# Ten weight loads without a product on TensorE after each round of attention heads and HGRN2

## The chip, the cores and the metric

The kernel runs on one core of a Trainium2 chip. The metric is the device time of one execution in microseconds (us): the median over several runs. TensorE has two clock levels, 2.4 GHz, which the profile calls a granted clock of 1.0, and 1.2 GHz, a granted clock of 0.5; a stretch that mixes them shows a value between.

## The reference

A hybrid model over 512 tokens of width 1024, all in float32. The first block has two layers; the second block (two more layers with gated feed-forward parts, pooling and dilated attention) isn't touched by the change. One layer of the first block:

```python
h = rmsnorm(x, norm1_g[l])
u = jnp.einsum('btd,de->bte', h, w_in[l])            # all projections at once
y_m = mlstm_mixer(mq, mk, mv, mo, mi, mf, ...)       # 4 heads
y_a = diff_attention(aq, ak, av, ...)                # 4 heads of two softmaxes, causal
y_h = hgrn2_mixer(hq, hf, hi, hg, ...)               # 4 heads, a gated linear recurrence
mix = jnp.concatenate([y_m, y_a, y_h], axis=-1)
x = x + jnp.einsum('bte,ed->btd', mix, w_out[l])
h2 = rmsnorm(x, norm2_g[l])
a = jnp.square(jax.nn.relu(jnp.einsum('btd,df->btf', h2, w_up[l])))
x = x + jnp.einsum('btf,fd->btd', a, w_down[l])
```

The differential attention takes, per head, two causal softmaxes of q k^T and applies their difference to v. HGRN2 is, per head, a product of q and k with a decay between the two positions, applied to v, plus the state carried from earlier positions.

## The kernel before

Everything is kept transposed, with channels on the 128 partitions and the 512 tokens along the free dimension, and the residual x stays on the chip. A dense projection is cut into units of weights of up to 128 x 2048 elements. Each weight is split into a high and a low part (ScalarE rounds at L577, GpSimd subtracts at L594), and TensorE makes three products per tile (L661, L662, L663) in place of one exact one. The five engines each run a program of their own, written out in order; they meet at semaphores only. What `self.pe.e` issues runs on TensorE in the order of issue. A float32 or bf16 product is issued as a weight load and a product, so each product brings its own weights. In the profile an exact float32 product issued by the helper `mm` (L418, its work at L419) shows as two records.

The order is made by Python generators. Each part of the model is a generator per engine that yields between its steps; `weave` (L258) takes so many steps of each of its streams per round and yields once per round; `often` (L289) goes through a generator and lets three of four steps end a round, so that it advances four steps in three rounds; `run` (L296) exhausts a generator. The same Python runs for all engines, each time with that engine's generators.

`mixers` (L2621) weaves two lines in each of the two layers. The first line ends the mLSTM and then runs attention heads 1 and 3 (`heads(1, ...)`). The second line first runs the last ten units of the input projection (`rest`), and when these are over it weaves heads 0 and 2 (`other_heads`) with `states`: HGRN2, and then the output projection (`out`). So from the end of `rest` on, heads 1 and 3, heads 0 and 2 and HGRN2 share the engines with no dense projection beside them, until `out` begins. On TensorE these are

- `pe_heads` (L1814): the reciprocal norms spread with `sel` (L1831), v turned to tokens (L1836), and for each of four query blocks the scores q k^T (L1846), a bf16 identity times a causal mask added to them (L1848), the weights turned (L1856), the weights times v (L1862); then sums with a column of ones (L1868) and factors spread (L1876);
- `pe_hgrn` (L2021): the values turned to tokens (L2034), q k^T (L2042), seven levels of decayed products (L2055, tiles called scr), the keys turned (L2068), the near part (L2076), the state carried over blocks (L2082, L2086), and the norm (`pe_rstd`, L1315).

VectorE and ScalarE do the steps between: for HGRN2 a level's product is copied under a mask by VectorE (L2154), and the decayed operand of a next one is made by VectorE (L2132, L2133, L2141, L2142) around an exponential on ScalarE (L2218); for the heads VectorE takes maxima (L1899) and combines the two softmaxes (L1908, L1911), and ScalarE takes the exponentials (L1964).

`ident16` (L409) is the bf16 identity, 128 x 128, made once at the start (L1216) and used as weights for the masks.

Of the kernel before, what the change touches and what calls it, by code (L numbers as in the profile page):

```python
# [257 lines left out]
def weave(*streams):  # L258

    streams = list(streams)  # L260
    while streams:
        for s in list(streams):
            for _ in range(s[1]):
                if next(s[0], s) is s:
                    streams.remove(s)
                    break
        yield


def every(n, steps):  # L270
    for i, _ in enumerate(steps):
        if i % n == n - 1:
            yield


def chain(*parts):
    for steps in parts:
        yield from steps


def beside(n, steps, *others):

    for i, _ in enumerate(steps):
        if i % n == n - 1:
            for line in others:
                next(line, None)


def often(steps):  # L289

    for i, _ in enumerate(steps):
        if i % 4 != 1:
            yield


def run(steps):  # L296
    for _ in steps:
        pass
# [19 lines left out]
class Kernel:  # L318
# [2299 lines left out]

    def mixers(self, l, rest, mlstm, heads, hgrn, out):  # L2621


        first = PHASES[f"in_ah{l}"].first
        mine = FIRST_BANK[first + PHASES[f"in_ah{l}"].count]
        self.heads_begun = False
        self.heads_left = 2

        def first_line():
            yield from mlstm  # L2630
            while self.unit < first + 6:
                yield
            self.heads_begun = True
            yield from heads(1, (5, 6, 7))
            self.heads_left -= 1

        def states():
            yield from hgrn((mine, mine + 1))
            for i, _ in enumerate(out):
                yield  # L2640

                while i == 11 and self.heads_left:
                    yield

        def other_heads():
            yield from heads(0, (2 - mine, 3 - mine, 4))
            self.heads_left -= 1

        def second_line():
            yield from every(3, rest)  # L2650
            line = states()
            while not self.heads_begun:
                yield next(line)
            yield from weave((other_heads(), 1), (often(line), 1))
        run(weave((first_line(), 1), (second_line(), 1)))

    def tensor(self):
        self.pe_start()
        for l in range(DEPTH):
            mlstm = self.pe_mlstm(l)  # L2660
            beside(3, chain(self.pe_dense(f"in_m{l}"), self.pe_dense(f"gates{l}"), self.pe_dense(f"in_n{l}")), mlstm)
            self.mixers(l, self.pe_dense(f"in_ah{l}"), mlstm, lambda n, banks: self.pe_heads(l, n, banks),
                        lambda banks: self.pe_hgrn(l, banks), self.pe_dense(f"out{l}"))
            for g in range(2):
                run(self.pe_dense(f"up{l}{g}"))
                run(self.pe_dense(f"down{l}{g}"))
        for name in ("gateupa0", "backa0", "gateupa1", "backa1"):
            run(self.pe_dense(name))
        self.pe_post_norm()
        for name in ("pool_in", "pool_out"):  # L2670
            run(self.pe_dense(name))
            if name == "pool_in":
                self.pe_last_groups()
        self.pe_post_norm()
        for name in ("gateupb0", "backb0", "gateupb1", "backb1"):
            run(self.pe_dense(name))
        self.pe_post_norm()
        for name in ("k", "v", "gateupc0", "backc0", "gateupc1", "backc1"):
            run(self.pe_dense(name))
        self.pe_post_norm()  # L2680
        self.attention_b(self.pe_dense("q"), self.pe_dilated)
        self.pe_weights()
        run(self.pe_dense("o"))
        self.pe_post_norm()
        for name in ("gateupd0", "backd0", "gateupd1", "backd1"):
            run(self.pe_dense(name))
        self.pe_post_norm()
        self.pe_store()
# [151 lines left out]
```

## Time and profile before

| | |
|---|---|
| median of 3 runs | 3642.12 us (3635.84 to 3644.48) |
| the profiled execution | 3640.93 us |
| its span | 3639.6 us |
| TensorE busy, its weight loads | 94%, 75% of the span |
| VectorE, ScalarE, GpSimd busy | 35%, 31%, 34% |
| chain of waits: TensorE, VectorE, ScalarE | 85%, 9%, 3% |
| mean granted clock | 0.953 |

The profile is one execution. Its page gives the busy time of each engine, the same in 40 equal slices with the granted clock, the DMA queues, the chain of work that ended last and the costliest groups of instructions. The trace behind it was asked for windows (busy time in a stretch), the timeline (instructions in order of time), the waits and the chain of a stretch. PE is TensorE's products and PEld its weight loads, which overlap the products; DVE is VectorE, ACT ScalarE, POOL GpSimd, and L419 is line 419.

### The profile page before, as it was taken

How to read it: one execution, taken by the hardware profiler on the slowest of the kernel's cores; microseconds unless marked ns; L12 is line 12 of the kernel's file. 1: busy time of each engine (PE TensorE's matmuls, PEld its weight loads, DVE VectorE, ACT ScalarE, POOL GpSimd, SP SyncE). 2: the span in 40 equal slices, each digit the busy share in tenths (PEclk: the TensorE clock that was granted, in tenths of full speed). 3: DMA queues.
4: the chain of work that ended last, by engine and by line, in shares of the span. 5: the costliest groups of instructions: out<-in, count | busy, mean ns of one | idle time of the engine just before them, and what ended most of it. 6: DMA issues, size and time to landing. Idle time of an engine off the chain costs nothing.

```text
span 3639.6 us, 37143 instructions
## 1 busy us (share of the span) xinstructions
PE 3403.8 (94%) x15674; PEld 2725.1 (75%) x15674; DVE 1256.4 (35%) x2031; ACT 1139.0 (31%) x1557; POOL 1223.6 (34%) x299
## 2 busy tenths in 40 slices
PE   7996799999987999999998999999999989769999
PEld 5675588887755788888887778887888867658887
DVE  5336531314356421222123441123221243662122
ACT  3234432323234432322223332223221233433222
POOL 4220144443210344444444324443444432024442
PEclk9996899999987899999999999999999999879998
DMA  4110023332210133333333223333433323023332
GB/s 125 58 58 1 24 94 104 93 93 84 63 35 1 59 103 93 93 94 97 99 91 104 78 70 93 104 93 114 140 91 102 89 81 110 12 58 93 100 93 74
DMA packets 461820, 296.76 MB, mean 82 GB/s; under 512 B 14296, under 2 KB 454158, under 8 KB 461598
## 3 DMA queue, kind: packets, MB, share of 16 engines
q1 hardware_dynamic: 453664, 277.09, 26.2%
q10 hardware_dynamic: 7990, 17.30, 1.4%
q8 instruction: 123, 2.02, 0.3%
q14 instruction: 43, 0.35, 0.0%
HBM read 285.97 MB, written 8.39 MB: 81 GB/s over the span
## 4 chain that ended last, share of the span: by engine, by line
PE 85%; DVE 9%; ACT 3%; POOL 1%; issue 1%; DMA 0%; SPq 0%; DVEq 0%; ACTq 0%; POOLq 0%
PE bank L661 24%; PE bank L662 24%; PE bank L663 24%; PE bank L419 9%; PE bank L703 1%; PE bank L704 1%; PE bank L705 1%; DVE scr L2154 1%; DVE ta L1513 1%; DVE x L1120 1%; DVE ta L1118 1%; POOL wlo L594 0%; DVE qkv L2432 0%; DVE ta L2429 0%; DVE tb L2430 0%
## 5 line engine op out<-in xcount | busy, mean ns | idle before, releaser
L594 POOL TENSOR_TENSOR wlo<-raw,whi 128x2048 fp32r<-128x2048 f32 (+3 forms) x278 | 1178.3, 4239 | 2331.8 <-ACT whi L577 2331.8
L661 PE MATMUL bank<-xh,whi 128*128 128x512 f32 x2304 | 916.8, 398 | 23.2 <-DVE xl L1144 15.3
L663 PE MATMUL bank<-xh,wlo 128*128 128x512 f32 x2304 | 900.4, 391 | 0.0
L662 PE MATMUL bank<-xl,whi 128*128 128x512 f32 x2304 | 900.3, 391 | 0.0
L577 ACT ACTIVATE whi<-raw 128x2048 fp32r<-128x2048 f32 (+3 forms) x280 | 493.9, 1764 | 585.1 <-PE bank L663 547.3
L661 PEld LDWEIGHTS bank<-xh,whi 128*128 128x128 f32 x2304 | 434.7, 189 | 141.7 <-issue 32.2
L663 PEld LDWEIGHTS bank<-xh,wlo 128*128 128x128 f32 x2304 | 434.2, 188 | 92.6
L662 PEld LDWEIGHTS bank<-xl,whi 128*128 128x128 f32 x2304 | 435.1, 189 | 87.5 <-issue 1.4
L661 PE MATMUL bank<-ah,whi 128*128 128x512 f32 x1216 | 474.1, 390 | 5.2 <-POOL wlo L594 5.2
L662 PE MATMUL bank<-al,whi 128*128 128x512 f32 x1216 | 473.8, 390 | 0.0
L663 PE MATMUL bank<-ah,wlo 128*128 128x512 f32 x1216 | 473.6, 389 | 0.0
L850 DVE TENSOR_TENSOR ta<-bank,rs 128x512 f32<-128x512 f32 x176 | 120.9, 691 | 594.7 <-PE bank L663 594.4
L661 PEld LDWEIGHTS bank<-ah,whi 128*128 128x128 f32 x1216 | 228.7, 188 | 53.5 <-POOL wlo L594 6.0
L663 PEld LDWEIGHTS bank<-ah,wlo 128*128 128x128 f32 x1216 | 228.7, 188 | 47.8
L662 PEld LDWEIGHTS bank<-al,whi 128*128 128x128 f32 x1216 | 228.7, 188 | 47.3
L661 PE MATMUL bank<-mh,whi 128*128 128x512 f32 x480 | 188.1, 392 | 9.6 <-DVE ml L1649 9.6
L1083 ACT ACTIVATE ah<-ta 128x512 fp32r<-128x512 f32 x88 | 55.9, 635 | 433.5 <-DVE ta L854 433.5
L662 PE MATMUL bank<-ml,whi 128*128 128x512 f32 x480 | 187.7, 391 | 0.0
L663 PE MATMUL bank<-mh,wlo 128*128 128x512 f32 x480 | 187.7, 391 | 0.0
L832 DVE TENSOR_TENSOR x<-bank,x 128x512 f32<-128x512 f32 x48 | 33.2, 691 | 313.8 <-PE bank L663 313.8
L419 PE MATMUL bank<-u 64*128 64x128 f32 (+5 forms) x576 | 104.7, 387 | 26.0 <-ACT u L2211 16.4
L1080 ACT ACTIVATE tb<-ta 128x512 f32<-128x512 f32 x88 | 55.7, 633 | 224.3 <-DVE ta L850 224.2
(378 smaller groups left out, 3227.0 us busy)
## 6 DMA issues: line engine op xcount, KB each, us to landing
raw<-in_ffn_w_gate SPq DMA_DIRECT2D x85, 512.0 KB, 4.0
raw<-in_ffn_w_up SPq DMA_DIRECT2D x85, 512.0 KB, 5.2
raw<-in_w_up SPq DMA_DIRECT2D x64, 512.0 KB, 4.7
raw<-in_w_down SPq DMA_DIRECT2D x64, 512.0 KB, 5.1
raw<-in_w_in SPq DMA_DIRECT2D x56, 512.0 KB, 4.8
raw<-in_ffn_w_down SPq DMA_DIRECT2D x64, 384.0 KB, 4.1
raw<-in_ffn_w_down SPq DMA_DIRECT2D x64, 320.0 KB, 3.8
raw<-in_w_out SPq DMA_DIRECT2D x16, 512.0 KB, 4.4
```

Of the source, the lines that this page charges most:

```text
L419: return self.pe.e.matmul(out, lhsT, rhs, start=start, stop=stop, skip_group_check=True)
L577: a.e.activation(self.whi[slot][:, 0:n], self.raw[slot][:, 0:n], ACT.Copy).then_inc(self.hi_made.tick(u), 1)
L594: g.e.tensor_tensor(self.wlo[slot][:, 0:n], self.raw[slot][:, 0:n], self.whi[slot][:, 0:n].bitcast(F32), ALU.subtract).then_inc(self.lo_ma ...
L661: pe.e.matmul(bank, hi[:, at:at + P], xh, start=k == ks[0], stop=False)
L662: pe.e.matmul(bank, hi[:, at:at + P], xl, start=False, stop=False)
L663: last = pe.e.matmul(bank, lo[:, at:at + P], xh, start=False, stop=k == ks[-1])
L703: pe.e.matmul(bank, hi[:, at:at + P], xh, start=k == 0, stop=False)
L704: pe.e.matmul(bank, hi[:, at:at + P], xl, start=False, stop=False)
L705: last = pe.e.matmul(bank, lo[:, at:at + P], xh, start=False, stop=k == ph.nk - 1)
L850: v.e.tensor_tensor(r[:], bank[:], self.rs[:], ALU.mult).then_inc(read, 1)
L1080: a.e.activation(self.tb[0][:], self.ta[0][:], ACT.Silu).then_inc(self.part_a.tick("silu", u), 1)
L1083: a.e.activation(self.ah[:, j, :], self.ta[1][:], ACT.Copy).then_inc(self.part_a.tick("hi", u), 1)
```

## The change

After each round of the outer weave of `mixers`, if HGRN2 has begun and has not ended, TensorE loads the bf16 identity as weights ten times. No product follows these loads. Only TensorE's program passes the function in; for the other engines `between` is None and `alone` has no effect.

```diff
+    def pe_keep_awake(self):
+        for _ in range(10):
+            self.pe.e.ldweights(self.ident16())
+
-    def mixers(self, l, rest, mlstm, heads, hgrn, out):
+    def mixers(self, l, rest, mlstm, heads, hgrn, out, between=None):
...
         self.heads_left = 2
+        self.alone = False
...
         def states():
+            self.alone = True
             yield from hgrn((mine, mine + 1))
+            self.alone = False
             for i, _ in enumerate(out):
                 yield
...
-        run(weave((first_line(), 1), (second_line(), 1)))
+        for _ in weave((first_line(), 1), (second_line(), 1)):
+            if between and self.alone:
+                between()
...
             self.mixers(l, self.pe_dense(f"in_ah{l}"), mlstm, lambda n, banks: self.pe_heads(l, n, banks),
-                        lambda banks: self.pe_hgrn(l, banks), self.pe_dense(f"out{l}"))
+                        lambda banks: self.pe_hgrn(l, banks), self.pe_dense(f"out{l}"), self.pe_keep_awake)
```

## Rows read from the trace of the kernel before

**Rows 1.** The page: span, busy time, slices, instruction loading, the chain by engine.
```profile
span 3639.6 us, 37143 instructions
PE 3403.8 (94%) x15674; PEld 2725.1 (75%) x15674; DVE 1256.4 (35%) x2031; ACT 1139.0 (31%) x1557; POOL 1223.6 (34%) x299
...
PEclk9996899999987899999999999999999999879998
...
q8 instruction: 123, 2.02, 0.3%
...
PE 85%; DVE 9%; ACT 3%; POOL 1%; issue 1%; DMA 0%; SPq 0%; DVEq 0%; ACTq 0%; POOLq 0%
```

**Rows 2.** Windows of both stretches: length, busy time per engine, granted clock, DMA.
```profile
core 0: us, PE busy (x) PEld busy (x) DVE busy (x) ACT busy (x) POOL busy (x), PEclk, DMA share, GB/s
266.30:420.30 154.00, 105.98 (x633) 75.50 (x632) 94.58 (x234) 67.22 (x146) 0.00 (x0) 0.70 0.00 1
1051.10:1205.20 154.10, 106.06 (x633) 75.03 (x632) 94.58 (x234) 67.21 (x146) 0.00 (x0) 0.71 0.00 1
```

**Rows 3.** The chain within 266.3 to 420.3 us: shares, then start, length, what.
```profile
by line: PE bank L419 39.6%; DVE scr L2154 7.4%; DVE tiny L1899 4.3%; issue 4.3%; DVE u L1911 3.8%; PE bank L1856 3.3%; PE bank L1836 2.5%; DVE scr L2142 2.1%; ACT scr L2218 2.0%; DVE tiny L1908 1.9%; DVE scr L2141 1.6%; DVE scr L2132 1.6%;
...
293.71 6.14 PE bank L419 x40
```

**Rows 4.** TensorE's longest wait within 266.3 to 420.3 us: total, times, longest.
```profile
PE bank L419 <- DVE scr L2154: 19.9, 9, 4.8
```

**Rows 5.** Timeline of the products: start, length, what, in brackets idle time before.
```profile
293.71 2.08 PE L419 MATMUL bank<-scr 64*128 64x128 f32 x16 [1.26 <-DVE scr L2154]
295.72 2.07 PE L419 MATMUL bank<-u 128*128 128x128 f32 x8
297.73 2.08 PE L419 MATMUL bank<-scr 64*128 64x128 f32 x16
299.60 0.96 PE L419 MATMUL bank<-u 64*128 64x384 f32 x4
...
301.77 1.16 PE L419 MATMUL bank<-scr 64*128 64x128 f32 x16
307.69 0.59 PE L419 MATMUL bank<-scr 64*128 64x128 f32 x2 [4.76 <-DVE scr L2154]
```

**Rows 6.** The same at the end of the first stretch.
```profile
420.35 0.77 PE L661 MATMUL bank<-mh,whi 128*128 128x512 f32 x1 [4.81 <-DVE ml L1649]
```

**Rows 7.** Loads of the bf16 identity: timeline; then all, min/median/max in ns.
```profile
286.32 0.11 PEld L419 LDWEIGHTS bank<-half 128*128 128x128 bf16 x2 [0.62 <-issue]
...
3030.19 0.45 PEld L419 LDWEIGHTS bank<-half 128*128 128x128 bf16 x8
...
3115.18 0.77 PEld L419 LDWEIGHTS bank<-half 128*128 128x128 bf16 x8 [0.22 <-issue]
...
L419 PEld LDWEIGHTS bank<-half x184: 95/98/152, 269.1 to 3183.5; 128*128 128x128 bf16 x184
```

**Rows 8.** Float32 loads with one-column products: timeline; then all, min/median/max in ns.
```profile
2472.44 0.97 PEld L419 LDWEIGHTS bank<-ones,tb 128*128 128x128 f32 x8 [0.74 <-ACT tb L1101]
...
L419 PEld LDWEIGHTS bank<-ones,tb x48: 186/192/337, 1966.1 to 3621.1; 128*128 128x128 f32 x48
```

**Rows 9.** Windows, as rows 2: three stretches, each followed by the one behind it.
```profile
404.70:409.10 4.40, 3.92 (x34) 3.80 (x33) 0.17 (x1) 3.15 (x5) 0.00 (x0) 1.00 0.02 4
409.20:413.30 4.10, 2.55 (x6) 1.17 (x7) 1.94 (x10) 3.82 (x7) 0.00 (x0) 0.50 0.00 0
381.90:385.90 4.00, 2.31 (x14) 0.83 (x12) 3.49 (x8) 2.29 (x7) 0.00 (x0) 1.00 0.00 0
386.00:392.80 6.80, 6.11 (x50) 4.97 (x50) 2.88 (x9) 2.07 (x6) 0.00 (x0) 1.00 0.00 1
2470.80:2474.10 3.30, 2.03 (x17) 1.83 (x15) 0.99 (x3) 2.12 (x3) 1.26 (x1) 1.00 0.21 50
2474.20:2477.50 3.30, 2.07 (x8) 1.78 (x8) 1.16 (x2) 0.00 (x0) 0.00 (x0) 0.50 0.75 261
```

## The prediction

> **What bounds the kernel now.** The page comes first [rows 1]: TensorE is busy for 94% of the span and the chain of work that ended last is 85% TensorE, nearly all of it dense projections at a granted clock of 1.0. The change touches none of those. The digits of the granted clock dip twice, at slices 3 to 4 and 11 to 13. The windows [rows 2] cut out the two stretches behind these dips, one per layer, in which the last attention heads and HGRN2 run with no projection beside them: 266.3 to 420.3 us and 1051.1 to 1205.2 us. In each, TensorE is busy for 106 of 154 us at a mean granted clock of 0.70 and 0.71, VectorE for 95. So the whole question lies in 308 of 3640 us, and the second stretch repeats the first to 0.1 us. The chain inside the first stretch [rows 3] gives TensorE 39.6 + 3.3 + 2.5 = 45%, and most of the rest is VectorE in short steps. TensorE idles for the other 48 of the 154 us; the largest part of that, 19.9 us in nine waits, is for VectorE's masked copies of HGRN2 [rows 4]. The stretch is bounded by a relay: a TensorE group, a VectorE group, a TensorE group. An extra microsecond on TensorE ahead of a group in that relay is a microsecond more; inside a wait it is free.
>
> **The change, part by part.** It removes and moves nothing. It adds ten weight loads of a bf16 identity after each round of the weave in which HGRN2 has started and not ended. It adds no wait, no semaphore, no DMA, and only TensorE's program has it.
>
> How many: HGRN2's TensorE generator yields 42 times for each of its two pairs of heads, 8 times in the norm and twice at its end, 94 in all. `often` takes four of its steps in three rounds, so this is 70 rounds. 70 x 10 = 700 loads per layer, 1400 in the run. The program grows by 1400 on 37143 instructions, 4%; instruction loading takes 0.3% of the DMA engines [rows 1], so I cost this at nothing, and nothing waits on that queue.
>
> Where they stand: I laid the rounds of the code beside TensorE's groups of the first stretch. 50 groups of products are issued in it, and the first dense product behind it makes 51. In front of 19 of the 51 TensorE waits at least 0.58 us; the other 32 follow the group ahead within 0.2 us. The groups of [rows 5] show the pattern: the scr group at 293.71 ends a round, a round with no product follows, so two rounds of loads (20) come before the u group at 295.72; one round comes before the u group at 299.60 and one before the scr group at 301.77, all three without idle time. Ahead of 307.69 stand two more rounds, and there TensorE idles 4.76 us for VectorE, which hides them. Over the stretch, 41 of the 70 rounds of loads stand ahead of the 32 groups with no idle time, and 29 fall into waits. For 25 of the 41 the chain of waits runs through TensorE at that moment (as in the piece of 6.14 us at 293.71 [rows 3], which holds the two and the one); at the other 16 it runs on VectorE or ScalarE. The last round falls into the 4.81 us wait ahead of the first output projection [rows 6].
>
> What one load costs: no row shows a load with no product behind it. The nearest [rows 7]: two bf16 loads start 15 ns apart, since the pair takes 0.11 us and one takes 0.10; eight with a product each take 0.45 us, so (0.45 - 0.10) / 7 = 50 ns on average, and the seven of steady pace are 56 ns apart, which the product sets; at the half clock eight take 0.77 us, 95 ns each. The median length of one is 98 ns. So a load takes between 15 ns (only its issue) and about 100 ns (its whole length, if each must end before the next begins). Below nothing is not possible for the load itself; a gain could come only through the clock, and that is a rival. I take 35 ns, the middle between 15 and the 56 at which a load and a product together run, because the rows at full clock already show loads overlapping: 98 ns long and 56 apart. Ten loads then cost 0.35 us.
>
> A rule of the Trainium skill bears on this. TensorE: Matmul & The Clock Gate, section LDWEIGHTS (loading the stationary operand), puts a load at its columns over 1.2 GHz; by it this would be an estimated 107 ns, the end of rival B. [...]
>
> The sum: 25 rounds on the chain paid in full, and half of the 16 off it (a late TensorE group there delays VectorE's in-order queue in some places and not in others), 33 x 0.35 = 11.6 us per layer, 23 us for both. No waited group overflows: the largest pile is three rounds, 1.05 us, ahead of waits of 1.7 us and more. From 420.3 us on everything keeps its pace, only later. The profiled execution took 3640.9 us, 1.2 under the median of 3642.1. **3640.9 + 23.1 = 3664 us.**
>
> **Rivals.**
>
> A, the forecast, over its load prices of 25 to 56 ns: from 25 x 0.25 x 2 = 12.5 to 41 x 0.56 x 2 = 46 us, so 3653 to 3687 us.
>
> B, loads in series: with no product between them each waits for the last. Then ten cost 1.0 us. The 25 rounds on the chain plus what overflows the short waits come to 27 us per layer, all 41 plus the overflow to 43: 3696 to 3726 us. It speaks for it that a bf16 load is 95 ns long at the least [rows 7]; against it that f32 loads with one-column products, which add next to no product time, come eight in 0.97 us though one is 192 ns long, so they start (0.97 - 0.19) / 7 = 111 ns apart and overlap [rows 8].
>
> C, the loads nearly free: at 15 ns ten cost 0.15 us, 25 x 0.15 x 2 = 7.5 us, and some of that is absorbed where VectorE is late anyway. 3641 to 3652 us, mostly inside the noise. For it: the issue spacing in [rows 7].
>
> D, faster: the loads keep the granted clock at its upper level (2.4 GHz) through the stretch. A scr group of 16 takes 2.08 us at 0.5 and 1.16 us at 1.0 [rows 5], 44% less. TensorE has 45% of 154 us on the chain, 70 us, of which 60% runs at 0.5 (mean clock 0.70): 42 x 0.44 = 18.5 us per layer, 37 for both, less 7 to 28 us for the loads: 3611 to 3632 us. Against it stand [rows 9]. From 404.7 to 409.1 us TensorE counts as busy for 3.92 of 4.4 us, with loads for 3.80 of them, 16 of the 34 products having one column; the stretch behind it runs at 0.5. From 381.9 to 385.9 it is busy for 2.31 of 4.0 us, with loads for 0.83 but longer products, and the stretch behind it stays at 1.0. From 2470.8 to 2474.1, 15 loads in 1.83 us with one-column products, behind dense work at 1.0, end at 0.5. So products hold the clock, and loads alone did not. These loads are f32; a bf16 load might count otherwise, and that is what is left of D. The same page of the Trainium skill, Part 1, says that the clock follows how busy the engine was and advises against idle gaps; read plainly, that gives D, and these rows speak against that reading for weight loads.
>
> E, the change doesn't do what it says, because `alone` is set too early or late: it is false while the projections run and true from HGRN2's first step on, so I give this nothing.
>
> **How the numbers follow.** A 57%, C 18%, B 15%, D 10%. The predicted time is A's, 3664 us. The range goes from 3640 (C with everything absorbed) to 3708 (the middle of B); outside lie D and half of B, 18%. A measurement of this kernel can tell about 0.3%, 11 us, from no change: D is faster (0.09 with its small end left out), C and the lowest edge of A are the same (0.22), the rest is slower (0.69).
>
> **What would show each step.** In the profile after: 1400 loads more from the identity at the new line, and TensorE's count of products unchanged. The spacing of ten loads in a row: 0.35 us says A, 0.15 C, 1.0 B. The two stretches longer by 11 to 12 us each and the time between them unchanged at 631 us. The mean granted clock still 0.68 to 0.73 in both; 0.9 or more would be D. TensorE's waits for the masked copies shorter by some 0.35 to 0.7 us each, not gone. The prediction is wrong if the stretches are shorter, if the loads cost over 60 ns each, or if a stretch grows by less than 8 us at loads of 35 ns, which would mean that VectorE's relay absorbs more than I gave it.

## The result and the profile after

The changed kernel takes 3674.87 us (median of 3 runs, 3673.54 to 3677.03) against 3642.12 us before: ratio 1.0092, 95% interval 1.0078 to 1.0107, 33 us slower. Forecast were 3664 us, range 3640 to 3708. The direction and the range hold; of the 33 us the prediction's sum had 23.

The page of the profile after, the lines that answer to [rows 1]:

```profile
span 3673.6 us, 38543 instructions
PE 3431.1 (93%) x15674; PEld 2798.2 (76%) x17074; DVE 1256.8 (34%) x2031; ACT 1138.7 (31%) x1557; POOL 1223.6 (33%) x299
...
PEclk9996799999976899999999999999999999879999
...
q8 instruction: 129, 2.11, 0.3%
```

1400 loads more and not one product more, and yet TensorE's products are busy for 27 us longer. The same work takes longer, and that was not in the forecast. The windows of the two stretches and of the dense work between them and behind them, columns as in [rows 2]:

```profile
core 0: us, PE busy (x) PEld busy (x) DVE busy (x) ACT busy (x) POOL busy (x), PEclk, DMA share, GB/s
267.40:437.50 170.10, 118.38 (x632) 110.29 (x1324) 94.44 (x234) 67.62 (x146) 0.00 (x0) 0.63 0.00 1
437.60:1066.20 628.60, 620.48 (x2720) 489.56 (x2729) 204.03 (x271) 197.66 (x227) 231.58 (x51) 0.99 0.29 85
1066.20:1236.30 170.10, 118.44 (x632) 110.33 (x1325) 94.50 (x234) 67.63 (x146) 0.00 (x0) 0.63 0.00 1
1236.40:3673.60 2437.20, 2339.27 (x10696) 1918.65 (x10696) 750.39 (x1120) 721.78 (x929) 909.48 (x220) 0.97 0.31 91
```

Each stretch grew from 154 to 170 us, 16 us each, 32 for both; the time between them is 2 us shorter and the time behind them 3 us longer. VectorE's and ScalarE's busy times are those of before. TensorE's products in the stretch are busy for 118 us in place of 106, and the mean granted clock is 0.63 in both, where it was 0.70 and 0.71.

The loads themselves, all of them and then four rows of the timeline in the part that answers to [rows 5]:

```profile
L2623 PEld LDWEIGHTS <-half x1400: 95/102/181, 266.9 to 1230.2; 128*128 128x128 bf16 x175
...
298.59 0.99 PEld L2623 LDWEIGHTS <-half 128*128 128x128 bf16 x20 [0.22 <-issue]
303.54 0.53 PEld L2623 LDWEIGHTS <-half 128*128 128x128 bf16 x10 [0.22 <-issue]
307.66 0.51 PEld L2623 LDWEIGHTS <-half 128*128 128x128 bf16 x10
...
331.26 0.46 PEld L2623 LDWEIGHTS <-half 128*128 128x128 bf16 x10
```

Ten loads take 0.46 us where the clock is 1.0 and 0.53 where it is 0.5; without the length of the last, (0.46 - 0.10) / 9 = 40 ns and (0.53 - 0.10) / 9 = 47 ns from start to start. A round of ten loads so takes TensorE 0.40 to 0.47 us, 0.44 on average. The products around them:

```profile
296.58 2.08 PE L419 MATMUL bank<-scr 64*128 64x128 f32 x16
299.53 2.08 PE L419 MATMUL bank<-u 128*128 128x128 f32 x8 [0.87 <-issue]
301.53 2.08 PE L419 MATMUL bank<-scr 64*128 64x128 f32 x16
304.08 1.65 PE L419 MATMUL bank<-u 64*128 64x384 f32 x4 [0.47 <-issue]
...
308.19 1.16 PE L419 MATMUL bank<-scr 64*128 64x128 f32 x16 [0.23 <-issue]
313.70 1.66 PE L419 MATMUL bank<-scr 64*128 64x128 f32 x12 [4.35 <-DVE scr L2154]
```

Both prices are in these rows. Where [rows 5] has no idle time, TensorE's products now stand apart by 0.87 us behind two rounds of loads and by 0.47 and 0.23 us behind one ("issue": it waits for nothing but its own queue). And the u group at 304.08 takes 1.65 us where it took 0.96: before, the clock had risen to 1.0 by then, now it is still 0.5. The wait for VectorE at the end has shrunk from 4.76 to 4.35 us. The wait of 1.26 us that stood ahead of the first group of [rows 5] is gone: that group, now at 296.58, follows without idle time. Over the stretch the waits of [rows 4] shrank from 19.9 us in nine to 14.8 us in seven, and issue became a line of its own:

```profile
PE bank L419 <- DVE scr L2154: 14.8, 7, 4.3
PE bank L419 <- issue: 6.5, 17, 0.9
```

Laid product by product beside the stretch before, the growth splits into three parts: 12 us more in which products are busy (118 in place of 106), about 12 us more idle time at places where there had been little or none, and about 8 us less at the places where TensorE had waited 0.55 us or more. The first part comes with the lower clock, since the products are the same; the second is the loads; the third says that the waits took back a good part of both. That is bookkeeping on one timeline, and it doesn't say from which of the two the waits took. Which loads are on the path, and what the clock takes, needed experiments.

### The profile page after: what moved, and what is told of

Read it like the earlier page. It is cut to its first block, busy times and chain, and to the rows that moved or that the text cites. A ratio compares the mean times of both kernels' runs of the same rounds, so it can differ in the third digit from the quotient of the medians.

```text
span 3673.6 us, 38543 instructions
## 1 busy us (share of the span) xinstructions
PE 3431.1 (93%) x15674; PEld 2798.2 (76%) x17074; DVE 1256.8 (34%) x2031; ACT 1138.7 (31%) x1557; POOL 1223.6 (33%) x299
## 4 chain that ended last, share of the span: by engine, by line
PE 86%; DVE 9%; ACT 3%; issue 1%; POOL 1%; DMA 0%; SPq 0%; DVEq 0%; ACTq 0%; POOLq 0%
PE bank L661 24%; PE bank L662 24%; PE bank L663 24%; PE bank L419 10%; PE bank L703 1%; PE bank L704 1%; PE bank L705 1%; DVE ta L1513 1%; DVE x L1120 1%; DVE ta L1118 1%; POOL wlo L594 0%; DVE scr L2154 0%; DVE qkv L2432 0%; DVE ta L2429 0%; DVE tb L2430 0%
## 5 line engine op out<-in xcount | busy, mean ns | idle before, releaser
L419 PE MATMUL bank<-u 64*128 64x128 f32 (+5 forms) x576 | 114.0, 417 | 33.4 <-ACT u L2211 12.4
```

Source lines behind the costliest of these rows:

```text
L419: return self.pe.e.matmul(out, lhsT, rhs, start=start, stop=stop, skip_group_check=True)
```

## The experiments

Two theories stood against each other. The first: a load costs 40 to 47 ns where TensorE has no wait to put it in, and besides the loads thin out the products (they leave fewer of them in a given time), so that the granted clock is at 0.5 for longer. The rival: the loads' own time is all. Unless it is said otherwise the edit is to the changed kernel, and all kernels compute the full result.

### How the cost grows with the number

```diff
-        for _ in range(10):
+        for _ in range(5):      # five_loads
+        for _ in range(20):     # twenty_loads
```

> Five loads after each round in place of ten. Theory 1 (loads of 40 to 47 ns on TensorE's path, and a lower granted clock because the products stand thinner): the 41 rounds ahead of groups without idle time cost 0.20 to 0.24 us each, 8 to 10 us per layer; 2 to 4 of it are absorbed and the clock costs up to 5: 12 to 26 us slower than before in all. Rival (only the loads' own time counts, the clock costs nothing): half of the 33 us of ten loads, 16 us.

> Twenty loads after each round. Theory 1: 41 rounds x 0.80 to 0.94 us = 33 to 39 us per layer, the short waits overflow by 1 to 2 us, the clock costs about the 5 us that it costs with ten, and 4 to 5 us are absorbed: 65 to 80 us slower than before, and the time at the half clock longer again. Rival (only the loads' own time): twice 33 us, 66 us, with the time at the half clock growing only as the stretch does.

Five loads: ratio 1.0040 (1.0028 to 1.0053), 14 us. Twenty: 1.0204 (1.0188 to 1.0219), 73 us. With 33 us for ten this is nearly a straight line, so it can't tell the theories apart; both had forecast it. The windows of the stretches do more. Of five loads, then of twenty:

```profile
267.40:428.10 160.70, 113.17 (x632) 92.59 (x977) 94.53 (x234) 67.33 (x146) 0.00 (x0) 0.67 0.00 1
1059.40:1216.70 157.30, 107.88 (x632) 88.56 (x979) 94.27 (x234) 67.26 (x146) 0.00 (x0) 0.71 0.00 1
```

```profile
267.70:457.30 189.60, 124.78 (x632) 147.23 (x2012) 94.04 (x233) 68.00 (x146) 0.00 (x0) 0.58 0.00 1
1086.40:1276.40 190.00, 124.30 (x632) 146.10 (x2013) 94.06 (x233) 67.88 (x146) 0.00 (x0) 0.59 0.00 1
```

The two stretches with five loads hold the same instructions, and the one at 0.67 is 3.4 us longer than the one at 0.71, with 5.3 us more of busy products. The executions show it too: the two of 3647 and 3648 us have a mean clock of 0.953 over the whole kernel, three of the other four, 3656 to 3660 us, 0.946. With twenty the clock of the stretches falls to 0.58 and 0.59. So time goes with the clock and the clock with the number of loads, which is what the first theory says and the rival doesn't. But the stretch at 0.71 also has five loads after each round: with so few the clock can stay where it was before, and that stretch is only 3.2 us longer than before.

### Where the loads stand

```diff
+        n = 0
         for _ in weave((first_line(), 1), (second_line(), 1)):
             if between and self.alone:
-                between()
+                between(n)
+                n += 1
...
+        if n in self.WAITED:       # loads_in_waits, 29 rounds
+        if n not in self.WAITED:   # loads_no_idle, 41 rounds
+        if n in self.OFF:          # loads_off_chain, 16 of the 41
```

> Ten loads only after the 29 rounds of 70 per layer behind which TensorE waits anyway. Theory 1: they are hidden, 0 +/- 4 us against the kernel before, and the granted clock of both stretches stays at 0.70. Rival (each round of loads costs the same wherever it stands): 33 x 29 / 70 = 14 us slower. Rival (loads in the waits hold the clock): faster by 10 us or more, granted clock above 0.75.

> Ten loads only after the 41 rounds per layer behind which TensorE goes on without waiting. Theory 1: nearly the whole of the change, 28 to 34 us slower than before, granted clock near 0.63 in both stretches. Rival (each round costs the same wherever it stands): 33 x 41 / 70 = 19 us slower.

> Ten loads only after the 16 rounds per layer that stand ahead of groups without idle time, at moments when the chain of waits runs on VectorE or ScalarE. The prediction counted half of them: 16 x 0.43 us x 0.5 = 3.4 us per layer, 7 us in all. Rival (off the chain is free): 0 +/- 3 us. Rival (every round ahead of a group without idle time pays in full): 16 x 0.43 = 6.9 us per layer, 14 us in all.

The 29 rounds ahead of waits: ratio 1.0000 (0.9990 to 1.0010). They are 580 more instructions, so a longer program alone costs nothing that can be seen. The 41 others: 1.0097 (1.0082 to 1.0112), 33 us by the medians, the whole change. The 16 of those at moments when the chain of waits is on another engine: 1.0005 (0.9996 to 1.0014), nothing clear of noise, where the expectation had 7 us. The first stretch of that kernel:

```profile
266.30:420.30 154.00, 106.81 (x633) 81.82 (x792) 94.44 (x234) 67.42 (x146) 0.00 (x0) 0.70 0.00 1
```

It has the length and the clock of before. A load costs by its place. By subtraction the 25 rounds per layer on the chain carry the whole cost; a kernel with only these wasn't run. An estimate of their own time is 25 x 0.44 = 11 us per layer, 22 us in all. It leaves 11 of the 33 us that aren't the loads' own time.

The two stretches of the kernel with loads in waits happen to differ by their clock:

```profile
267.90:418.40 150.50, 101.31 (x633) 84.39 (x922) 94.02 (x233) 67.02 (x146) 0.00 (x0) 0.74 0.00 1
1046.70:1200.70 154.00, 106.15 (x633) 87.36 (x923) 94.65 (x234) 67.19 (x146) 0.00 (x0) 0.71 0.00 1
```

The same work and the same hidden loads, 3.5 us apart at 0.74 and 0.71. This pair and that of five_loads give about 1 us of time for 0.01 of clock. From 0.70 or 0.71 down to 0.63 this would be an estimated 7 to 8 us per stretch, 14 to 16 in all, more than the 11 us left over by the subtraction. One pair speaks against so firm a price: the stretches of loads_no_idle have clocks of 0.66 and 0.63 (the expectation had 0.63 for both) and are equally long, 170 us.

### Does a load count for the clock?

First at the end of each stretch, behind the last round, where the clock is 0.5:

```diff
+        if n == 69:
+            for _ in range(80):     # end_loads
+                self.pe.e.ldweights(self.ident16())
...
+        if n == 69:
+            for _ in range(50):     # end_products
+                self.pe.e.matmul(self.bank[6][:, 3 * P:4 * P], self.ident16(), self.ident16(),
+                                 start=True, stop=True, skip_group_check=True)
```

> No loads but 80 in one row, after the last round of each stretch, inside the wait ahead of the first output projection. Theory 1 (a load doesn't hold the granted clock): 3.2 to 3.8 us of loads, hidden, and the clock is 0.5 when the output projection begins, as before: 0 +/- 3 us. Rival (bf16 loads count as much as products): the clock is 1.0 when it begins, and the some 6 us at 0.5 there are gone, 2 to 3 us per layer faster.

> At the same place 50 bf16 products of the identity with itself, 128 columns each, into a bank that nobody reads at that time, in place of the loads. Theory 1 (products hold or raise the clock, loads don't): 2.8 to 5.4 us of products in the same wait, the clock is 1.0 when the output projection begins, 2 to 6 us faster than before in all. Rival (nothing done there changes the clock, since the engine idled too long ahead of it): 0 +/- 3 us.

Windows of end_loads: the burst, then the product behind it.

```profile
412.40:416.20 3.80, 0.22 (x1) 3.66 (x79) 2.13 (x3) 2.01 (x3) 0.00 (x0) 0.50 0.00 0
416.30:418.50 2.20, 2.07 (x2) 0.53 (x3) 0.04 (x1) 0.43 (x1) 0.00 (x0) 0.50 0.00 0
```

The same of end_products:

```profile
412.40:416.60 4.20, 4.20 (x49) 4.06 (x49) 2.13 (x3) 2.41 (x3) 0.00 (x0) 0.62 0.00 0
416.80:418.30 1.50, 1.18 (x5) 0.29 (x2) 0.29 (x1) 0.00 (x0) 0.00 (x0) 1.00 0.00 0
```

Eighty loads in 3.8 us leave the clock at 0.50, and the two product records behind them take 2.07 us. Fifty products in 4.4 us raise it to 1.0, and the same two take 1.12 us. The products' burst is a little longer, but that isn't the reason: the mean of 0.62 over the window of 4.2 us says that the clock was up for its last 1.0 us, from 415.6 us on, and the loads of the other kernel ran until 416.3 us. Neither gained time: 1.0005 (0.9996 to 1.0014) with loads, and with products 1.0017 (1.0008 to 1.0026), which is 6 us slower and outside of what either theory had forecast. The expectation was wrong about the place. The last round ends between the two last spreading products of HGRN2's norm and not behind both, so the burst delayed the second by 3.7 to 4.4 us, and the clock was back at 0.5 when the output projection began. The wait ahead of that projection shrank from 4.81 to 3.12 us in both, which hid part of it. In the products' profile the second output projection starts only 1 us later than before (1206.1 against 1205.3 us); most of the 6 us lie behind it, in work that the edit doesn't touch:

```profile
1205.30:3639.60 2434.30, 2335.48 (x10696) 1915.68 (x10696) 750.32 (x1120) 722.56 (x929) 909.57 (x220) 0.97 0.31 91
1206.10:3645.20 2439.10, 2340.54 (x10696) 1919.93 (x10696) 750.16 (x1120) 721.74 (x929) 909.32 (x220) 0.97 0.31 91
```

These are the rest of the kernel before and of end_products: the same products, 5 us more of busy time and 5 us more in length. Even ahead of the burst the clock differs for the same instructions: from 266.3 to 412.0 us it is 0.71 in the kernel before and 0.75 in both of these. So the clock also differs where the edits do nothing, and a few us of any of these totals can be that.

Then inside the stretch, in waits, with the clock at 1.0. Both leave out the ten loads per round and put a number of their own ahead of the waits that they fit into:

```diff
+    def product(self, bank):
+        self.pe.e.matmul(self.bank[bank][:, 3 * P:4 * P], self.ident16(), self.half[:, 4, :],
+                         start=bank != 7, stop=bank != 7, skip_group_check=True)
...
+        bank, count = self.FILL.get(n, (0, 0))     # products_in_waits: 36 ahead of the longest wait
+        for _ in range(count):
+            self.product(bank)
...
+        for _ in range(self.FILL.get(n, 0)):       # loads_for_products: 50 there
+            self.pe.e.ldweights(self.ident16())
```

`half[:, 4, :]` is a tile of zeros, made at the start; the bank is one that only TensorE touches at that time.

> No loads; bf16 products of 128 columns (identity times zeros) in waits of the stretch alone, sized to them: 20 ahead of the wait of 2.9 us, 36 ahead of 4.9 us, 4 to 22 ahead of eleven others, 50 at the end; a third of the waits can't be filled, since all banks are in use. What is computed stays the same. Theory 1: the granted clock of both stretches rises from 0.70 to 0.80 or more and the kernel becomes faster, by 10 to 30 us. Rival (the clock costs nothing here since VectorE sets the pace): within 5 us of before, whatever the clock.

> The first set of products in waits with each count replaced by 1.4 times as many loads, so that they fill the waits for the same time at 40 ns each (50 loads ahead of the wait of 4.9 us), and none at the end. Theory 1: the clock falls in these waits as before (the group behind the longest wait takes 2.08 us, at 0.5), 0 +/- 4 us. Rival (loads hold a clock that is already up, even if they can't raise it): that group takes 1.16 us, as with products, and the kernel is faster by 5 us or more.

Timeline of products_in_waits, then the loads and the group behind them of loads_for_products:

```profile
302.73 2.18 PE L2630 MATMUL bank<-half 128*128 128x128 bf16 x36
307.48 1.16 PE L419 MATMUL bank<-scr 64*128 64x128 f32 x16 [2.57 <-DVE scr L2155]
```

```profile
303.02 2.06 PEld L2625 LDWEIGHTS <-half 128*128 128x128 bf16 x50
...
307.77 2.08 PE L419 MATMUL bank<-scr 64*128 64x128 f32 x16 [4.68 <-DVE scr L2154]
```

2.2 us of products in the wait hold the clock at 1.0, and the scr group behind it takes 1.16 us; 2.1 us of loads in the same wait don't, and it takes 2.08 us, as in the kernel before. The kernels: loads_for_products 0.9998 (0.9989 to 1.0007), products_in_waits 0.9990 (0.9981 to 0.9999). The latter was expected to gain 10 to 30 us and gained 2 to 4, though its clock rose to 0.74 in both stretches. At the point that the kernel before reaches at 411.8 us it was 3.8 us ahead; then the 50 products at the end took 5.51 us ahead of the second spreading product, and the first output projection started only 0.5 us earlier than before.

### The loads with the clock held up, and the better fill

```diff
+        bank, count = self.FILL.get(n, (0, 0))
+        for _ in range(count):
+            self.product(bank)
+        if n not in self.WAITED:       # products_and_loads; not in more_products_in_waits
+            for _ in range(10):
+                self.pe.e.ldweights(self.ident16())
```

> The same products in waits, and the ten loads after each of the 41 rounds per layer ahead of groups without idle time. It gives the price of the loads at a clock held up. Theory 1: 20 to 30 us slower than the products in waits alone, less than the 33 us that the loads cost without them, since loads start 40 ns apart at the upper clock and 47 at the lower, and nothing more is lost to the clock. Rival (the clock takes no part in the 33 us): 33 us slower than the products alone.

> As the products in waits, without the 50 at the end (which stood ahead of the last spreading product and not in the wait behind it) and with more in the other waits: 62 ahead of the longest, 36, 34 and 8 to 22 ahead of the others. Theory 1 (products hold the clock, a us at the upper clock is worth about a third of a us of time): 8 to 15 us faster than before, clock of both stretches 0.76 or more. Rival (what the clock gives, the added products take): within 4 us of before.

Products in waits and loads in the 41 other rounds: 3663.8 us, 24 us by the medians and 27 us by the ratios over the products in waits alone, where the same loads cost 33 to 35 us without them. Its four runs lie between 3658.5 and 3670.6 us, and the profiled one is the slowest. Windows of the stretches, of products_in_waits and then of this kernel:

```profile
266.30:419.80 153.50, 116.97 (x855) 86.83 (x854) 94.20 (x234) 66.75 (x146) 0.00 (x0) 0.74 0.00 1
1047.90:1201.50 153.60, 117.00 (x855) 86.84 (x855) 94.26 (x234) 66.81 (x146) 0.00 (x0) 0.74 0.00 1
...
268.90:433.30 164.40, 125.70 (x854) 107.70 (x1255) 94.42 (x234) 67.14 (x146) 0.00 (x0) 0.71 0.00 1
1065.00:1232.00 167.00, 126.38 (x854) 108.30 (x1256) 94.53 (x234) 67.33 (x146) 0.00 (x0) 0.70 0.00 1
```

The test was meant to price the loads at a clock held up. It didn't hold it up: the loads took it from 0.74 to 0.70 and 0.71, so the 24 to 27 us have some of the clock in them too. Against the first theory's forecast of 20 to 30 us and the rival's 33 they speak for the first, but they don't split the cost. Between the subtraction (11 us) and the pairs of equal stretches (14 to 16 us, an estimate), the clock took roughly a third to a half of the 33 us, and the loads' own time the rest.

More products, and none at the end: 3627.43 us, ratio 0.9960 (0.9948 to 0.9973), 14 us faster than the kernel before and 47 us faster than the changed one. Its stretches, and the longest wait:

```profile
266.80:413.50 146.70, 112.57 (x897) 83.68 (x896) 93.80 (x234) 66.76 (x146) 0.00 (x0) 0.77 0.00 1
1041.60:1188.30 146.70, 112.61 (x897) 83.71 (x896) 93.83 (x234) 66.79 (x146) 0.00 (x0) 0.77 0.00 1
...
303.27 3.64 PE L2630 MATMUL bank<-half 128*128 128x128 bf16 x62
308.02 1.16 PE L419 MATMUL bank<-scr 64*128 64x128 f32 x16 [1.11 <-DVE scr L2155]
```

154 to 147 us each. So the clock can be raised and time gained, with products in place of loads and in waits only. The products went into 12 of the 29 rounds ahead of waits, into banks that no other engine used at that time.

### What a load's price goes by

```diff
-            self.pe.e.ldweights(self.ident16())
+            self.pe.e.ldweights(self.half[:, 0, 0:32])     # narrow_loads
```

> The change with loads of 32 columns in place of 128. If a load's price is the fixed spacing of 40 ns in the queue, the same as with 128 columns: 33 us slower than before. If it goes with the columns (or what is read): a quarter, 5 to 12 us slower. The loads hold the clock in neither case by theory 1, near 0.63 to 0.70.

Ratio 1.0032 (1.0022 to 1.0041), 9 to 12 us; its ten runs spread from 3647 to 3662 us. Rows of its timeline and of all its loads:

```profile
266.48 0.34 PEld L2623 LDWEIGHTS <-half 128*32 128x32 bf16 x10 [1.50 <-issue]
268.32 0.39 PEld L2623 LDWEIGHTS <-half 128*32 128x32 bf16 x10
...
324.09 0.26 PEld L2623 LDWEIGHTS <-half 128*32 128x32 bf16 x10
...
L2623 PEld LDWEIGHTS <-half x1400: 92/93/163, 266.5 to 1204.2; 128*32 128x32 bf16 x175
```

A load of 32 columns is as long as one of 128, 93 against 102 ns, but the next starts sooner: mostly 15 to 20 ns later at a clock of 1.0 (the row at 324.09: (0.26 - 0.09) / 9 = 19 ns) and 27 ns later at 0.5 (the row at 266.48), and not 40 and 47. Between the two forms the length hardly changes and the spacing does, though not in proportion to the columns.

## Why the prediction was right in direction and short in size

**The place of the question** held: 32 of the 33 us arose in the two stretches, and the dense work kept its pace to 3 us.

**The number and the places** held in the main: 1400 loads, no product more, the 29 rounds ahead of waits free (1.0000), the 41 others the whole cost (1.0097). Three readings were off. The last round doesn't fall into the 4.81 us wait ahead of the output projection but stands ahead of the second spreading product, which now waits 0.46 us for its loads. One wait with three rounds ahead of it is 1.50 us and not 1.7 or more; its 30 loads took 1.46 us and just fitted. And the waits for masked copies didn't all shrink by 0.35 to 0.7 us: the longest did (4.76 to 4.35 us), but two of the nine are gone, one of them 1.26 us long.

**The price of a load** was taken as 35 ns and is 40 to 47. Taking the middle between the issue spacing and the spacing of load and product together [rows 7] was 20% too low; a value nearer to the pair's 56 ns would have been right. The bounds of 15 and 100 ns held it. Over the 25 rounds of both layers this is 4 to 5 us (22 in place of 17.5).

**The half of the 16 rounds off the chain** was wrong. Nothing clear of noise was paid for them (loads_off_chain, 1.0005). The chain of waits had said so, and the prediction hedged against it. This overstated the sum by 16 x 0.5 x 0.35 x 2 = 5.6 us, and it was luck that this hid part of the two terms that were too low.

**The clock** is the step that failed. The prediction weighed whether loads would hold it and rightly said no; [rows 9] had told this, and the bursts at the end and in the long wait confirm it for bf16 loads. From this it went on to a clock unchanged at 0.68 to 0.73 and put its cost at nothing. Measured was 0.63. Where the loads lay off the chain or in waits (loads_off_chain, loads_in_waits) the clock stayed at 0.70 or above; where they stood on the chain it fell, to 0.66 and 0.63 with ten and to 0.58 with twenty. So the thinning of the products is the likely reason. What it cost is a third to a half of the 33 us, by estimates that don't agree better than that. A stretch that already moves between both clock levels has no fixed clock to put into a sum.

So the corrected sum is up to 25 x 0.44 x 2 = 22 us for loads and 11 us or more for the clock. That it comes to the measured 33 proves nothing, since the 11 is what the subtraction left.

**The rivals.** B, loads in series at 1.0 us for ten, is refuted by the spacing. C, nearly free, by the same. D, loads hold the clock, is refuted by the bursts; that a higher clock is worth time was right: products, which do hold it, won 14 us by going from 0.70 to 0.77. The Trainium skill, TensorE: Matmul & The Clock Gate, Part 1, advises against idle gaps; what these runs add is that a gap filled with weight loads still let the clock fall (loads_for_products, 2.08 us for the group behind) or left it low (end_loads, 0.50). For the load itself, the Trainium skill's section LDWEIGHTS (loading the stationary operand) on that page gives an estimated 107 ns. Its section Weight-path perf modes has a faster way to load 128 columns that aren't fp32, with 4 times the speed as the theory for fp8 and about 2 times as measured on trn2; the latter makes an estimated 53 ns. The length of a load in the trace, 102 ns, is near the first figure, and the spacing of 40 to 47 ns is somewhat below the last.

**What stays open.** Why the spacing is 40 to 47 ns for 128 columns wasn't tried further. How the 33 us split between the loads' own time and the clock isn't settled: no run held the clock while the loads stood on the chain, and none had loads in the 25 rounds alone. How much of the clock's fall is chance can't be told from single profiles either. The same kernel's two stretches differ by 3.4 and 3.5 us (five_loads, loads_in_waits), and untouched work by 5 us between kernels (end_products), so each of these splits is good to a few us.

## What to carry to other kernels

Ask of each added instruction whether the chain of waits runs through its engine at that place: 45 of the 70 rounds here were free when tested by themselves, and the cost lay in the 25 others. Where TensorE's granted clock already moves between its two levels, treat it as a result of the change and not as a constant: what spreads the products out can cost twice, once by its own time and once by slower products. To keep the clock up in a wait, fill it with products into an idle bank, sized to the wait, and not with weight loads; here that was worth 14 us of 3641, where the change made the kernel 33 us slower.

## What the runs showed of the hardware

- bf16 weight loads with no product behind them start 40 ns apart at a clock of 1.0 and 47 ns at 0.5 with 128 columns, 15 to 27 ns with 32, though each is 93 to 102 ns long in the trace.
- 80 such loads in 3.8 us left the granted clock at 0.5, and 50 in 2.1 us didn't hold it at 1.0. 50 products of 128 columns in 4.4 us raised it, and 36 in 2.2 us, with zeros as the moving operand, held it.
- The same instructions took 157.3 us at a mean granted clock of 0.71 and 160.7 us at 0.67 (five_loads), 150.5 us at 0.74 and 154.0 us at 0.71 (loads_in_waits). But 170 us at both 0.66 and 0.63 (loads_no_idle).
- The clock isn't the same for the same instructions: from 266.3 to 412.0 us it was 0.71 in the kernel before and 0.75 in end_loads and end_products, whose edits act only later.
